# Query projection in half tiles inside the linear attention block, modulation slabs inside the attention projection

## The chip, the cores and the metric

One core of one Trainium2 chip runs the whole program in one launch. The metric is the device time in microseconds (us) of that core. TensorE (PE in the profile) multiplies, VectorE (DVE) and ScalarE (ACT) work elementwise, GpSimd (POOL) too, and SyncE (SP) issues most DMAs. Each engine runs its own queue of instructions in order; semaphores are the only order between queues.

## What is computed

Two layers over 640 tokens (512 latent, 128 context), model width 1024. Of one layer, as the reference has it, this matters here:

```python
mod = jax.nn.silu(cond) @ p['w_mod'][l] + p['b_mod'][l]
sh1, sc1, g1, sh2, sc2, g2 = jnp.split(mod, 6, axis=-1)
h = rms_norm(x, p['norm1'][l]) * (1.0 + sc1) + sh1
(gq, gk, gv, lq, lk, lv, lr, lgo, dq, dk, dv, merge) = split_columns(h @ p['w_in'][l])
gq = rms_norm(gq.reshape(b, n, GQA_HEADS, HEAD_DIM), p['gqa_q_norm'][l])   # gk, dq, dk likewise, then rotary
# A: grouped-query attention of gq, gk, gv; C: differential attention of dq, dk, dv
# B: gated linear attention of lq, lk, lv in chunks of 64 tokens, both directions:
#    state' = decay * state + k_to_end^T v;  out = (masked q_dec k_inv^T) v + q_dec state
gla_out = rms_norm(o_gla, p['gla_out_norm'][l]) * jax.nn.silu(lgo)
mixed = sum_i(sigmoid(merge_i) * (branch_i @ w_branch_i)) @ p['w_out'][l]
x = x + g1 * mixed          # then h from norm2, sc2, sh2; SwiGLU FFN; x = x + g2 * ffn
```

## The kernel before

Every product is made in three passes: a weight slab (2048 columns wide, 1 MB) is loaded into one of two slots of `raw`, ScalarE copies it to a rounded high part `wH`, VectorE subtracts to get the low part `wL`, and TensorE multiplies low activation by high weight, high by low and high by high. The program goes in blocks with a barrier of all engines between them: `head` (or `tail` of the layer before), then per layer `gla`, `project_attention`, `attention`, `merge`, `tail`.

`gla` does the chunked linear attention. The work is four units (`UNITS`: two head pairs by two directions) and, over them, ten steps a (head pair a // 5, token tile a % 5). TensorE first transposes the decayed keys (L703), ScalarE copies them to rows (`g_ker`, L652). `state_steps(u)` (L719) makes the chunk increments of unit u in PSUM banks 0 to 2, and VectorE's `chain(u)` (L825) runs the recurrence over them. `scores(a)` (L736), VectorE's `mask(a)` (L838), `outputs(a)` (L748, L760), VectorE's `out(a)` (L845) make one token tile. ScalarE takes squares (L668) and the square root, VectorE multiplies by the gate (`gate`, L862). TensorE's queue is written out by hand: scores(a + 1), outputs(a), with the four state steps, and in between eight modulation slabs `mod` (L419: 1 MB of `w_mod` each, the columns for g1 and sh2) and four `turn`s (L776) that bring two slabs' rows to columns; ScalarE copies the rows (L660), VectorE adds the bias (L439). After step 9, TensorE runs five half tiles of the first query slab (`row_part`, L344: 4 of 8 contraction tiles, 12 matmuls 512 wide) into banks 0 to 4; their slab is split during step 8 (L308, L313), the second one at the end (L697, L898).

`project_attention` (L903) projects nine slabs s = 0 to 8 (gq halves 0 and 1, dq halves 2 and 3, gk and gv together 4, dk halves 5 and 6, dv halves 7 and 8); s = 0 is already done. A part-1 slab completes five token tiles, which ScalarE copies from PSUM (L1014). Seven `units` of heads are normalised and rotated: ScalarE `squares(q)` (L998, L1003), VectorE `norm(q)` (L1043 to L1078). TensorE transposes them (L1116, table `turns`), ScalarE copies them back (L1024). `high` (L280) and `low` (L286) split the slab ahead. All four queues are loops over s, so what stands later in a step waits for all that is ahead of it: VectorE does low(s + 1), then the norms of `units_at[s]` = {1: (0), 2: (1), 3: (2), 4: (3, 4), 6: (5), 7: (6)}; ScalarE does high(s + 1), the copies of the five tiles, then the squares. At the start, SP spills the residual x to HBM (L945, 2.5 MB), and ScalarE's queue issues the rope tables and the caches; GpSimd makes eight products of the tables, which norm 0 waits for.

Of the kernel before, what the change touches and what calls it, by code (L numbers as in the profile page):

```python
# [21 lines left out]
F32 = mybir.dt.float32  # L22
# [3 lines left out]
ALU = mybir.AluOpType  # L26
# [92 lines left out]
class Stages:  # L119


    def __init__(self, nc, ctx):
# [57 lines left out]
        self.gmod = [at(f"gmod{j}", [P, KT, W256], x) for j, x in enumerate((61440, 69632, x0 + 51200))]  # L180
        self.gmrow = at("gmrow", [P, 512], x0 + 59392)
        self.g_s = [at(f"g_s{u}", [P, NCH, P], x) for u, x in enumerate((77824, 94208, 86016, 104448))]
        self.g_ker = at("g_ker", [P, 4, TT, P], x1)
# [401 lines left out]
MOD_BUF = [1, 0, 2, 1, 0, 2, 1, 2]  # L585


def load_gla_mod(sp, m, d, L, j, sem):
    sp.dma_start(m.gmod[MOD_BUF[j]][:, :, :], k_tiles(d["w_mod"], L, (8 + j) * W256, W256)).then_inc(sem, 16)


def gla(nc, m, d, L, nxt, ahead):
# [10 lines left out]
    with m.block() as block:  # L603
        @block.sync
        def _(sp):
            def load(j):
                load_gla_mod(sp, m, d, L, j, m.sem(f"mod_loaded{MOD_BUF[j]}"))

            def store(u):
                hp, dr = UNITS[u]  # L610
                sp.wait_ge(m.sem("state_done"), u + 1)
                sp.dma_start(d["new_state_gla"][0, ds(L, 1), dr, 2 * hp:2 * hp + 2, :, :].
                             rearrange("a h k e -> (a h k) e"), m.g_s[u][:, blank[dr], :]
                             ).then_inc(m.sem(f"state_out{u // 2}"), 16)

            for j in range(ahead):
                sp.sem_inc(m.sem(f"mod_loaded{MOD_BUF[j]}"), 16)
# [6 lines left out]
            for j in (3, 4, 5):  # L624
                sp.wait_ge(m.sem("slab_used"), j - 2)
                load(j)
            store(0)
            store(1)
            next_load(sp, m, nxt, 0, "slab_used", 5)
            for j in (6, 7):  # L630
                sp.wait_ge(m.sem("slab_used"), j - 1)
                load(j)
            next_load(sp, m, nxt, 1, "slab_used", 7)
            store(2)
            store(3)
            next_loaded(sp, m, nxt)
            next_load(sp, m, nxt, 2, "next_low", 1)
            sp.wait_ge(m.sem("next_loaded2"), nxt[2])
            sp.wait_ge(m.sem("state_out0"), 32)
            sp.wait_ge(m.sem("state_out1"), 32)  # L640
# [8 lines left out]
        def _(act):  # L649
            for u in range(4):  # L650
# [5 lines left out]
            def rows(p):  # L656
                act.wait_ge(m.sem("slab_used"), 2 * p + 2)
                if p:
                    act.wait_ge(m.sem("mod_turned"), p)
                nc.scalar.activation(m.gmrow[:, :], m.ps[:, 3, :], ACT.Copy).then_inc(m.sem("mod_rows"), 1)  # L660
# [16 lines left out]
            rows(0)  # L677
            squares(0, 0)
            squares(0, 1)
            rows(1)  # L680
            squares(0, 2)
            squares(0, 3)
            rows(2)
            squares(0, 4)
            std(0)
            act.wait_ge(m.sem("state_out0"), 32)
            next_high(nc, m, act, nxt, "o_done", 5)
            squares(1, 0)
            squares(1, 1)
            rows(3)  # L690
            for tt in range(2, TT):
                squares(1, tt)
            std(1)
            act.wait_ge(m.sem("next_loaded1"), nxt[2])
            act.wait_ge(m.sem("o_done"), 2 * TT)
            act.wait_ge(m.sem("state_out1"), 32)
            nc.scalar.activation(m.wH[:, 1, :], m.raw[:, 1, :], ACT.Copy).then_inc(m.sem("next_high"), 1)  # L697

        @block.tensor
        def _(pe):  # L700
# [65 lines left out]
            def mod(p):  # L766
                if p:
                    pe.wait_ge(m.sem("mod_added"), p)
                for j in (2 * p, 2 * p + 1):
                    pe.wait_ge(m.sem(f"mod_loaded{MOD_BUF[j]}"), 16 * (MOD_BUF[:j + 1].count(MOD_BUF[j])))  # L770
                    mod_groups(nc, m, m.gmod[MOD_BUF[j]], 3, (j % 2) * W256).then_inc(m.sem("slab_used"), 1)

            def turn(p):
                pe.wait_ge(m.sem("mod_rows"), p + 1)
                for t in range(4):
                    last = nc.tensor.matmul(m.ps[:, 3, 2 * t:2 * t + 2], m.gmrow[:, t * P:(t + 1) * P], m.sel[:, :],  # L776
                                            start=True, stop=True)
                last.then_inc(m.sem("mod_turned"), 1)
# [19 lines left out]
            for tt in range(TT):  # L798
                for sem, count in {0: (("state_done", 4), ("a_masked", 2 * TT)), 3: (("mod_added", 4),),
                                   4: (("o_summed", 2 * TT),)}.get(tt, ()):  # L800
                    pe.wait_ge(m.sem(sem), count)
                wh, wl = (w[:, 0, :].rearrange("p (k c) -> p k c", c=512) for w in (m.wH, m.wL))
                last = row_part(nc, m, wh, wl, tt, tt, 512, 0)
            last.then_inc(m.sem("next_half_done"), 1)

        @block.vector
        def _(dve):
# [40 lines left out]
            def add_mod(p):  # L848
                dve.wait_ge(m.sem("mod_turned"), p + 1)
                add_mod_bias(nc, m, L, 3, 16 + 4 * p, 4).then_inc(m.sem("mod_added"), 1)  # L850
# [44 lines left out]
            for tt in range(TT):  # L895
                gate(1, tt)
            dve.wait_ge(m.sem("next_high"), 2)
            nc.vector.tensor_tensor(m.wL[:, 1, :], m.raw[:, 1, :], m.wH[:, 1, :].bitcast(F32), ALU.subtract  # L898
                                    ).then_inc(m.sem("next_low"), 1)
            dve.wait_ge(m.sem("next_half_done"), 1)  # L900


def project_attention(nc, m, d, L):  # L903


    WIDE = 512
    slabs = [(C_GQ, WIDE, 0), (C_GQ, WIDE, 1), (C_DQ, WIDE, 0), (C_DQ, WIDE, 1), (C_GK, W256, 1),
             (C_DK, WIDE, 0), (C_DK, WIDE, 1), (C_DV, WIDE, 0), (C_DV, WIDE, 1)]
    n = len(slabs)
# [10 lines left out]
    units_at = {1: (0,), 2: (1,), 3: (2,), 4: (3, 4), 6: (5,), 7: (6,)}  # L920
# [14 lines left out]
    def load(sp, d, s, slot, sem):  # L935
        c0, cols, part = slabs[s]
        load_w_rows(sp, m, d, L, c0, cols, part, slot, sem)

    with m.block() as block:
        @block.sync  # L940
        def _(sp):
            out = m.sem("kv_stored")
            took_loads(sp, m)
            sp.sem_inc(m.sem("slab_loaded0"), 16)
# [19 lines left out]
            sp.wait_ge(m.sem("x_spilled"), 16)  # L964
# [11 lines left out]
        def _(act):  # L976
# [12 lines left out]
            def high(s):  # L989
                high_part(nc, m, act, s % 2, 16 * (s // 2 + 1), consumed(s - 2) if s > 1 else None)  # L990

            act.sem_inc(m.sem("high_ready"), 2)
# [14 lines left out]
            for s in range(n):  # L1007
                if 0 < s < n - 1:
                    high(s + 1)
                for tt in range(TT):  # L1010
                    t = 5 * group[s] + tt
                    if slabs[s][2]:
                        act.wait_ge(m.sem("tile_done"), t + 1)
                        nc.scalar.activation(place(s)[:, :, tt, :],  # L1014
                                             m.ps[:, t % 6, 0:slabs[s][1]].rearrange("p (b c) -> p b c", c=P),
# [20 lines left out]
        def _(dve):  # L1036
            order = Signal(m.sem("dve_order"))
            dve.sem_inc(m.sem("low_ready"), 2)  # L1038
# [44 lines left out]
            for s in range(n):  # L1083
                if 0 < s < n - 1:
                    low_part(nc, m, dve, s + 1, (s + 1) % 2)
# [4 lines left out]
        def _(pe):  # L1090
            turn = 0
            pe.sem_inc(m.sem("half_done"), 1)
            for s in range(1, n):
                pe.wait_ge(m.sem("low_ready"), s + 1)
                _, cols, part = slabs[s]
                for tt in range(TT):
                    t = 5 * group[s] + tt
                    if t >= 6:
                        pe.wait_ge(m.sem("tile_copied"), t - 5)
# [2254 lines left out]
```

## Time and profile before

| | |
|---|---|
| median of 3 runs | 2462.07 us (2461.62 to 2463.23) |
| profiled execution, span from first to last instruction | 2464.2 us |
| granted TensorE clock, mean | 0.980 |
| TensorE busy | 2354.2 us (96%) |
| VectorE, ScalarE, GpSimd busy | 1498.5, 1074.1, 218.1 us |
| DMA, mean | 91 GB/s |
| `gla`, layer 0 and layer 1 | from 151.4 and 1363.1 us to the projection's first matmul at 224.4 and 1431.2 |
| `project_attention`, layer 0 | 224.4 to 344.0 us |

The span leaves out what lies around the instructions of the execution; the page gives no other time of its own for it, and it lies 2.1 us above the median of the runs. A timeline row is: start in us, length in us, engine, line, operation, output<-input, shape, count, and in brackets the idle time of the engine before it and what ended it. A granted clock of 1.00 is 2.4 GHz, 0.50 is 1.2 GHz.

### The profile page before, as it was taken

Reading aid. Unit: us, or ns where it says so; the run is one execution under the profiler, and the core shown is the slowest. Engines: PE = TensorE matmul, PEld = TensorE weight load, DVE = VectorE, ACT = ScalarE, POOL = GpSimd, SP = SyncE. Lnnn points to the kernel's source line nnn. Section 1 sums busy time; section 2 is a strip of 40 time slices with the busy share of each in tenths; the row PEclk is TensorE's granted clock in tenths of the full one; section 3 lists DMA queues with packets and bytes.
Section 4 is the critical chain, followed back from the end, with each engine's and each line's share of the span. In section 5 each row is a group of like instructions: output and inputs, shape, how many; then the busy total and the mean of one; then the engine's idle time right before and its main releaser. Section 6 shows DMA issues by size and latency. Waiting matters only on the chain. (4 is left out here: it accounts for less than half of the span.)

```text
span 2464.2 us, 41036 instructions
## 1 busy us (share of the span) xinstructions
PE 2354.2 (96%) x16478; PEld 2181.3 (89%) x16478; DVE 1498.5 (61%) x2400; ACT 1074.1 (44%) x2129; POOL 218.1 (9%) x176
## 2 busy tenths in 40 slices
PE   6989989999999999999999899898999999999998
PEld 5867867789999899999998678677999989999998
DVE  3334656766665773755653446586776568557473
ACT  3533346744442552533435233576444335335252
POOL 1241000000002100000134110000000040000000
PEclk8989999999999999999999999999999999999999
DMA  8235223022225122332231441301222342323222
GB/s 244 88 99 182 70 87 129 27 70 77 89 83 184 48 86 69 86 103 69 78 102 54 148 144 38 102 1 43 78 78 78 111 129 77 96 69 96 59 82 82
DMA packets 248747, 224.03 MB, mean 91 GB/s; under 512 B 9040, under 2 KB 234384, under 8 KB 248048
## 3 DMA queue, kind: packets, MB, share of 16 engines
q1 hardware_dynamic: 242240, 218.59, 28.2%
q10 hardware_dynamic: 5808, 2.17, 0.4%
q8 instruction: 132, 2.16, 0.4%
q0 software_dynamic: 512, 0.66, 0.3%
q14 instruction: 55, 0.45, 0.1%
HBM read 211.70 MB, written 9.70 MB: 90 GB/s over the span
## 5 line engine op out<-in xcount | busy, mean ns | idle before, releaser
L2267 ACT ACTIVATE ring_high<-raw 128x512 fp32r<-128x512 f32 (+1 forms) x278 | 158.1, 609 | 254.0 <-PE ps L2626 146.6
L2411 DVE TENSOR_TENSOR ring_low<-raw,ring_high 128x512 fp32r<-128x512 f32 (+1 forms) x278 | 204.9, 763 | 74.1 <-ACT ring_high L2267 70.0
L2699 PE MATMUL ps<-hH,ring_low 128*128 128x320 f32 x640 | 197.9, 309 | 0.3
L2699 PE MATMUL ps<-hL,ring_high 128*128 128x320 f32 x640 | 197.8, 309 | 0.0
L2699 PE MATMUL ps<-hH,ring_high 128*128 128x320 f32 x640 | 197.8, 309 | 0.0
L1482 DVE SCALAR_TENSOR_TENSOR xT<-ps,mod,xT 128x512 f32<-128x512 f32 (+1 forms) x128 | 64.0, 546 | 189.2 <-PE ps L2626 189.2
L344 PE MATMUL ps<-wH,hL 128*128 128x512 f32 (+1 forms) x460 | 174.5, 379 | 4.8 <-DVEq L1038 3.6
L344 PE MATMUL ps<-wH,hH 128*128 128x512 f32 (+1 forms) x460 | 171.6, 373 | 0.0
L2626 PE MATMUL ps<-gH,ring_low 128*128 128x320 f32 x704 | 160.9, 310 | 0.3 <-DVE xT L1482 0.3
L2626 PE MATMUL ps<-gL,ring_high 128*128 128x320 f32 x704 | 160.4, 309 | 0.0
L2626 PE MATMUL ps<-gH,ring_high 128*128 128x320 f32 x704 | 160.4, 309 | 0.0
L2699 PE MATMUL ps<-t_high,ring_low 128*128 128x320 f32 x480 | 148.5, 309 | 1.8 <-ACT f_p L2315 1.8
L2699 PE MATMUL ps<-t_high,ring_high 128*128 128x320 f32 x480 | 148.3, 309 | 0.0
L2699 PE MATMUL ps<-t_low,ring_high 128*128 128x320 f32 x480 | 148.3, 309 | 0.0
L344 PE MATMUL ps<-wL,hH 128*128 128x512 f32 (+1 forms) x400 | 147.7, 369 | 0.0
L1382 DVE TENSOR_REDUCE a_st<-ps 128x2 f32<-128x1280 f32 x64 | 95.2, 1487 | 46.7 <-PE ps L1234 46.5
L2699 PEld LDWEIGHTS ps<-hH,ring_low 128*128 128x128 f32 x640 | 120.1, 188 | 0.7 <-issue 0.7
L2699 PEld LDWEIGHTS ps<-hH,ring_high 128*128 128x128 f32 x640 | 120.1, 188 | 0.0
L2699 PEld LDWEIGHTS ps<-hL,ring_high 128*128 128x128 f32 x640 | 120.1, 188 | 0.0
L2626 PEld LDWEIGHTS ps<-gH,ring_low 128*128 128x128 f32 x704 | 117.5, 188 | 0.5 <-DVE xT L1482 0.5
L2626 PEld LDWEIGHTS ps<-gL,ring_high 128*128 128x128 f32 x704 | 117.7, 188 | 0.0
L2626 PEld LDWEIGHTS ps<-gH,ring_high 128*128 128x128 f32 x704 | 117.7, 188 | 0.0
(381 smaller groups left out, 6307.8 us busy)
## 6 DMA issues: line engine op xcount, KB each, us to landing
raw<-in_w_in SPq DMA_DIRECT2D x56, 1024.0 KB, 5.2
raw<-in_w_ffn_in SPq DMA_DIRECT2D x88, 512.0 KB, 5.1
gmod<-in_w_mod SPq DMA_DIRECT2D x16, 1024.0 KB, 6.4
modw<-in_w_mod SPq DMA_DIRECT2D x16, 1024.0 KB, 5.3
raw<-in_w_ffn_out SPq DMA_DIRECT2D x16, 1024.0 KB, 5.3
b_raw<-in_w_branch SPq DMA_DIRECT2D x22, 512.0 KB, 3.9
head_w<-in_w_mod SPq DMA_DIRECT2D x8, 1024.0 KB, 12.3
raw<-in_w_out SPq DMA_DIRECT2D x8, 1024.0 KB, 6.3
```

The lines of the kernel that those rows point to most:

```text
L344: last = nc.tensor.matmul(m.ps[:, bank, 0:cols], tok(a[:, k0 + k, :], tt), w[:, k, :], start=(k0 + k == 0 and q == 0), stop=(k0 + k == KT ...
L1382: ins = nc.vector.tensor_reduce(m.a_st[:, s, 0:2], both(s), AX.X, ALU.max, negate=True)
L1482: ins = nc.vector.scalar_tensor_tensor(out=seg, in0=src[c], scalar=g, in1=seg, op0=ALU.mult, op1=ALU.add)
L2267: nc.scalar.activation(ring_block(m.ring_high, b, src.shape[1], src.shape[2]), src, ACT.Copy).then_inc(m.sem("w_high"), 1)
L2411: nc.vector.tensor_tensor(ring_block(m.ring_low, b, nk, cols), src, ring_block(m.ring_high, b, nk, cols).bitcast(F32), ALU.subtract).then_ ...
L2626: last = nc.tensor.matmul(m.ps[:, bank + h, 0:HALF], w[:, kk, :], a[:, k, h * HALF:(h + 1) * HALF], start=(k == 0 and q == 0), stop=(k == ...
L2699: last = nc.tensor.matmul(m.ps[:, plan.banks[n, 0][BANK[what]], 0:HALF], w[:, k, :], a[:, k, :], start=(first and k == 0 and q == 0), stop ...
```

## The change

The modulation slabs and their turns leave `gla` for `project_attention`. In their place, both halves of the first query slab pair (s = 0 and 1) run in `gla`, one half tile after each scores: `q_half(h)` is token tile h // 2, contraction half h % 2, all in PSUM bank 3, copied out by ScalarE's `q_rows`. Slabs 0 and 1 are loaded ahead of the block (in layer 0 only slab 0) and split at its start; slabs 2 and 3 are split at its end and slab 4 loaded. The projection begins with s = 2, has its tiles in banks 0 to 4 and the modulation in bank 5. The spill of x moves to the block before `gla`, so that x's memory can hold the states in `gla` and the modulation slabs in the projection.

```diff
 def gla
         @block.sync
-            for j in range(ahead, 3):
-                load(j)
...
+            for s in range(ahead, 2):
+                load_attention_slab(sp, m, d, L, s, m.sem(f"slab_loaded{s}"))
+            for s in (2, 3, 4):
+                sp.wait_ge(m.sem("slab_low"), s - 1)
+                load_attention_slab(sp, m, d, L, s, m.sem(f"slab_loaded{s}"))
+                if s == 3:
+                    for u in range(4):
+                        store(u)
+            sp.wait_ge(m.sem("slab_loaded4"), 16)
+            sp.wait_ge(m.sem("state_out"), 64)
         @block.scalar
+            def slab_high(s):
+                act.wait_ge(m.sem(f"slab_loaded{s}"), 16)
+                if s >= 2:
+                    act.wait_ge(m.sem("q_half_done"), 9 + s - 2)
+                nc.scalar.activation(m.wH[:, s % 2, :], m.raw[:, raw_slot(s), :], ACT.Copy).then_inc(m.sem("slab_high"), 1)
+
+            def q_rows(tt):
+                act.wait_ge(m.sem("q_half_done"), 2 * tt + 2)
+                nc.scalar.activation(m.rq[:, 0:4, tt, :], m.ps[:, 3, :].rearrange("p (b c) -> p b c", c=P), ACT.Copy
+                                     ).then_inc(m.sem("q_copied"), 1)
...
+            ker_rows(0)
+            ker_rows(1)
+            slab_high(0)
+            ker_rows(2)
+            ker_rows(3)
+            slab_high(1)
+            q_rows(0)
+            for a in range(2 * TT):
+                if a in (1, 3, 5, 7):
+                    q_rows((a + 1) // 2)
+                if a == 7:
+                    slab_high(2)
+                elif a == 8:
+                    slab_high(3)
+                squares(a // TT, a % TT)
+                if a % TT == TT - 1:
+                    std(a // TT)
         @block.tensor
+            def q_half(h):
+
+
+                tt, part = h // 2, h % 2
+                if h < 2:
+                    pe.wait_ge(m.sem("slab_low"), h + 1)
+                if part == 0:
+                    if tt:
+                        pe.wait_ge(m.sem("q_copied"), tt)
+                    else:
+                        pe.wait_ge(m.sem("ke_rows"), 2)
+                wh, wl = (w[:, part, :].rearrange("p (k c) -> p k c", c=512) for w in (m.wH, m.wL))
+                row_part(nc, m, wh, wl, tt, 3, 512, part).then_inc(m.sem("q_half_done"), 1)
 
             state_steps(0)
             scores(0)
-            mod(0)
-            turn(0)
+            q_half(0)
             state_steps(1)
+            q_half(1)
             for a in range(2 * TT):
                 if a + 1 < 2 * TT:
                     scores(a + 1)
+                if a < 8:
+                    q_half(a + 2)
                 outputs(a)
...
-                if a in (1, 3, 6):
-                    mod((1, 3, 6).index(a) + 1)
-                elif a in (2, 4, 7):
-                    turn((2, 4, 7).index(a) + 1)
-            pe.wait_ge(m.sem("next_low"), 1)
...
         @block.vector
+            slab_low(0)
             chain(0, range(9))
             mask(0)
-            add_mod(0)
+            slab_low(1)
             chain(1, range(9))
...
                 out(a)
-                if a in (2, 4, 7):
-                    add_mod((2, 4, 7).index(a) + 1)
-                elif a == 8:
-                    next_low(nc.vector, m, dve, nxt)
+                if a == 8:
+                    slab_low(2)
             gate(0, 4)
             done = inverse(1)
             dve.wait_ge(*done)
             for tt in range(TT):
                 gate(1, tt)
...
+            slab_low(3)
 def project_attention
-    units_at = {1: (0,), 2: (1,), 3: (2,), 4: (3, 4), 6: (5,), 7: (6,)}
+    units_at = {2: (0, 1), 3: (2,), 4: (3, 4), 6: (5,), 7: (6,)}
+    mod_at, turn_at = {(2, 0): 0, (2, 2): 1, (4, 0): 2, (4, 2): 3, (5, 0): 4, (5, 2): 5, (7, 0): 6, (7, 2): 7}, (2, 4, 5, 7)
         @block.sync
-            sp.dma_start(d["x_spill"], flat(m.xT[:, :, :])).then_inc(m.sem("x_spilled"), 16)
-            for s in range(3, n):
+            load_mod(0)
+            load_mod(1)
+            for s in range(5, n):
                 sp.wait_ge(m.sem("low_ready"), s - 1)
-                load(sp, d, s, s % 2, m.sem(f"slab_loaded{s % 2}"))
+                load_attention_slab(sp, m, d, L, s, m.sem(f"slab_loaded{raw_slot(s)}"))
+                for j in {5: (2, 3), 6: (4, 5), 7: (6, 7)}.get(s, ()):
+                    sp.wait_ge(m.sem("mod_used"), j - 1)
+                    load_mod(j)
         @block.scalar
-            for s in range(n):
-                if 0 < s < n - 1:
+            for s in range(begin, n):
+                if begin < s < n - 1:
                     high(s + 1)
                 for tt in range(TT):
                     t = 5 * group[s] + tt
+                    if s in turn_at and tt == 3:
+                        mod_rows(turn_at.index(s))
         @block.vector
+            for s in range(begin, n):
+                if begin < s < n - 1:
+                    low(s + 1)
+                if s - 1 in turn_at:
+                    p = turn_at.index(s - 1)
+                    dve.wait_ge(m.sem("mod_turned"), p + 1)
+                    add_mod_bias(nc, m, L, 5, 16 + 4 * p, 4).then_inc(m.sem("mod_added"), 1)
                 for q in units_at.get(s, ()):
                     norm(q)
         @block.tensor
+            def mod(j):
+                if j and j % 2 == 0:
+                    pe.wait_ge(m.sem("mod_added"), j // 2)
+                pe.wait_ge(m.sem(f"mod_loaded{j % 2}"), 16 * (j // 2 + 1))
+                mod_groups(nc, m, m.gmod[j % 2], 5, j % 2 * W256).then_inc(m.sem("mod_used"), 1)
...
+                    if (s, tt) in mod_at:
+                        mod(mod_at[s, tt])
+                    elif s in turn_at and tt == 4:
+                        turn_mods(turn_at.index(s))
```

## Rows read from the trace of the kernel before

**Rows 1.** The page's part 1: busy time, share of span, instructions of each engine.
```profile
PE 2354.2 (96%) x16478; PEld 2181.3 (89%) x16478; DVE 1498.5 (61%) x2400; ACT 1074.1 (44%) x2129; POOL 218.1 (9%) x176
```

**Rows 2.** Waits of TensorE, 60 to 350 us (layer 0): total, times, longest.
```profile
PE ps L1227 <- PEq L263: 5.4, 1, 5.4
PE ps L419 <- DMA gmod<-in_w_mod: 4.5, 2, 3.1
PE ps L748 <- DVE g_s L825: 2.3, 1, 2.3
```

**Rows 3.** The same waits, 1300 to 1560 us (layer 1).
```profile
PE ps L748 <- DVE g_s L825: 2.8, 1, 2.8
```

**Rows 4.** Timeline of TensorE, layer 0, last outputs and query half tiles: start, length, idle before.
```profile
208.20 0.28 PE L760 MATMUL ps<-g_s,u 64*64 64x128 f32 x2
...
209.08 0.50 PE L344 MATMUL ps<-wH,hL 128*128 128x512 f32 x1 [0.60 <-DVE wL L313]
...
224.43 0.47 PE L344 MATMUL ps<-wH,hL 128*128 128x512 f32 x1 [1.45 <-DVEq L1038]
```

**Rows 5.** Stretches of TensorE: length, busy (x), granted clock, DMA share, GB/s.
```profile
159.00:160.00 1.00, 0.19 (x4) 0.65 1.09 361
...
176.00:177.00 1.00, 1.00 (x10) 0.82 0.00 0
```

**Rows 6.** The same timeline earlier in the block: one length of each kind.
```profile
182.87 1.37 PE L719 MATMUL ps<-lv,g_ker 64*64 64x128 f32 x40 [0.43 <-DVE g_s L825]
184.17 1.05 PE L776 MATMUL ps<-sel,gmrow 128*128 128x2 f32 x8
185.15 0.49 PE L736 MATMUL ps<-u,u 64*128 64x128 f32 x4
...
185.80 1.16 PE L748 MATMUL ps<-lv,g_am 128*128 128x128 f32 x8
...
187.48 1.93 PE L419 MATMUL ps<-gmod,sc 128*32 128x256 f32 x32
```

**Rows 7.** Timeline of ScalarE: row copies and a wide copy; last row layer 1.
```profile
152.15 2.49 ACT L652 ACTIVATE g_ker<-ps 128x640 f32<-128x640 f32 x4 [1.72 <-PE ps L703]
...
194.62 1.89 ACT L308 ACTIVATE wH<-raw 128x2048 fp32r<-128x2048 f32 x1
...
1363.91 1.33 ACT L652 ACTIVATE g_ker<-ps 128x640 f32<-128x640 f32 x2 [2.42 <-PE ps L703]
```

**Rows 8.** Timeline of VectorE, layer 0: first and last wide work after the last copies.
```profile
206.75 2.28 DVE L313 TENSOR_TENSOR wL<-raw,wH 128x2048 fp32r<-128x2048 f32 x1
...
213.87 2.29 DVE L898 TENSOR_TENSOR wL<-raw,wH 128x2048 fp32r<-128x2048 f32 x1
```

**Rows 9.** Timeline of VectorE, layer 0: first state chain and the mask behind it.
```profile
155.10 2.65 DVE L825 SCALAR_TENSOR_TENSOR g_s<-g_s,g_dec,ps 128x128 f32<-128x128 f32 x7 [21.80 <-PE ps L719]
...
158.25 0.72 DVE L838 COPY_PREDICATED g_am<-g_cst,ps 128x512 f32<-128x512 int32 x1
```

**Rows 10.** The page's part 6: DMA issues, KB each, median us to landing.
```profile
raw<-in_w_in SPq DMA_DIRECT2D x56, 1024.0 KB, 5.2
```

**Rows 11.** Timeline of TensorE, layer 1: first matmul of the projection.
```profile
1431.19 0.47 PE L344 MATMUL ps<-wH,hL 128*128 128x512 f32 x1 [2.13 <-DVEq L1038]
```

**Rows 12.** Landing times of the modulation slabs' DMAs, from the view of their tile.
```profile
DMA to landing us min/median/max: 5.1/6.4/10.1
```

**Rows 13.** Stretches of TensorE behind two barriers, columns as in the fifth group.
```profile
1434.00:1436.00 2.00, 2.00 (x6) 0.53 1.07 451
...
353.00:354.00 1.00, 0.99 (x5) 0.57 1.08 362
```

**Rows 14.** Timeline of VectorE in the projection of layer 0: norm 2, low parts.
```profile
269.88 1.49 DVE L1043 TENSOR_REDUCE r_st<-r_sq 128x20 f32<-128x1280 f32 x1 [7.90 <-ACT r_sq L998]
...
278.44 2.29 DVE L286 TENSOR_TENSOR wL<-raw,wH 128x2048 fp32r<-128x2048 f32 x1
...
294.73 2.29 DVE L286 TENSOR_TENSOR wL<-raw,wH 128x2048 fp32r<-128x2048 f32 x1
```

More of the change, by code:

```diff
@@ L179, in __init__ @@
         self.g_e = [at(f"g_e{i}", [P, T], x1 + 2560 * i) for i in range(2)]
[L180 to L183, printed above, removed]
+        self.gmod = [at(f"gmod{j}", [P, KT, W256], 8192 * j) for j in range(2)]
+        self.gmrow = at("gmrow", [P, 512], 16384)
+        self.g_s = [at(f"g_s{u}", [P, NCH, P], 5120 * u) for u in range(4)]
+        self.g_ker = at("g_ker", [P, 4, TT, P], x0 + 51200)
         self.g_am = at("g_am", [P, 2, 2, 2, P], x1 + 10240)
@@ L582, in gate_scale, with attention_slabs, raw_slot, load_attention_slab @@
     nc.gpsimd.tensor_tensor(ki, m.lT[:, 2 + hp, :], ek, ALU.mult).then_inc(done, 1)
[L585 to L592, printed above, removed]
+def attention_slabs():
+    WIDE = 512
+    return [(C_GQ, WIDE, 0), (C_GQ, WIDE, 1), (C_DQ, WIDE, 0), (C_DQ, WIDE, 1), (C_GK, W256, 1),
+            (C_DK, WIDE, 0), (C_DK, WIDE, 1), (C_DV, WIDE, 0), (C_DV, WIDE, 1)]
+def raw_slot(s):
+    return (s + 1) % 2
+def load_attention_slab(sp, m, d, L, s, sem):
+    c0, cols, part = attention_slabs()[s]
+    load_w_rows(sp, m, d, L, c0, cols, part, raw_slot(s), sem)
+def spill_x(sp, m, d):
+    sp.dma_start(d["x_spill"], flat(m.xT[:, :, :])).then_inc(m.sem("x_spilled"), 16)
+def gla(nc, m, d, L, ahead):
     run = [list(range(0, 7)) + [8, 9], list(range(7, 0, -1)) + [9, 8]]
@@ L613, in store @@
                              rearrange("a h k e -> (a h k) e"), m.g_s[u][:, blank[dr], :]
-                             ).then_inc(m.sem(f"state_out{u // 2}"), 16)
-            for j in range(ahead):
-                sp.sem_inc(m.sem(f"mod_loaded{MOD_BUF[j]}"), 16)
+                             ).then_inc(m.sem("state_out"), 16)
+            for s in range(ahead):
+                sp.sem_inc(m.sem(f"slab_loaded{s}"), 16)
             for u, (hp, dr) in enumerate(UNITS):
@@ L649, in _, with ker_rows @@
         def _(act):
-            for u in range(4):
+            def ker_rows(u):
                 act.wait_ge(m.sem("ke_turned"), u + 1)
@@ L846, in out, with slab_low @@
                                       m.ps[:, 4:6, 0:P]).then_inc(m.sem("o_summed"), 1)
-            def add_mod(p):
-                dve.wait_ge(m.sem("mod_turned"), p + 1)
-                add_mod_bias(nc, m, L, 3, 16 + 4 * p, 4).then_inc(m.sem("mod_added"), 1)
+            def slab_low(s):
+                dve.wait_ge(m.sem("slab_high"), s + 1)
+                if s >= 2:
+                    dve.wait_ge(m.sem("q_half_done"), 9 + s - 2)
+                nc.vector.tensor_tensor(m.wL[:, s % 2, :], m.raw[:, raw_slot(s), :], m.wH[:, s % 2, :].bitcast(F32),
+                                        ALU.subtract).then_inc(m.sem("slab_low"), 1)
             def inverse(hp):
@@ L1092, in _, with turn_mods @@
             pe.sem_inc(m.sem("half_done"), 1)
-            for s in range(1, n):
+            pe.sem_inc(m.sem("tile_done"), TT)
+            def mod(j):
[3 more added lines that the diff above has]
+                mod_groups(nc, m, m.gmod[j % 2], 5, j % 2 * W256).then_inc(m.sem("mod_used"), 1)
+            def turn_mods(p):
+                pe.wait_ge(m.sem("mod_rows"), p + 1)
+                for t in range(4):
+                    last = nc.tensor.matmul(m.ps[:, 5, 2 * t:2 * t + 2], m.gmrow[:, t * P:(t + 1) * P], m.sel[:, :],
+                                            start=True, stop=True)
+                last.then_inc(m.sem("mod_turned"), 1)
+            for s in range(begin, n):
                 pe.wait_ge(m.sem("low_ready"), s + 1)
@@ L1097, in _ @@
                     t = 5 * group[s] + tt
-                    if t >= 6:
-                        pe.wait_ge(m.sem("tile_copied"), t - 5)
+                    if slabs[s][2] == 0 or slabs[s][1] == W256:
+                        pe.wait_ge(m.sem("tile_copied"), t - 4)
                     wh = m.wH[:, s % 2, :].rearrange("p (k c) -> p k c", c=cols)
                     wl = m.wL[:, s % 2, :].rearrange("p (k c) -> p k c", c=cols)
-                    last = row_part(nc, m, wh, wl, tt, t % 6, cols, part)
+                    last = row_part(nc, m, wh, wl, tt, t % TT, cols, part)
                     if part:
```

128 lines of the change are left out of this document (34 added, 94 removed).

## The prediction

> **What bounds the kernel now.** I read the page's busy times first: TensorE is busy 96% of the span [rows 1], so a change pays only where TensorE waits, or where it runs below its full clock. I then listed who TensorE waited for around the edited blocks. In layer 0 it loses 4.5 us to modulation slabs still in flight, 2.3 us to the first state chains and 5.4 us to the barrier behind the attention projection [rows 2]; in layer 1 the state chains cost 2.8 us [rows 3]. The barrier between the linear attention block (`gla`) and `project_attention` costs 1.45 us [rows 4]. These idle times, and one stretch in layer 0 in which the granted clock is down from 159.6 to 176.2 us [rows 5], are about all there is to win. The rest is the same work in another place.
>
> **Prices.** In the TensorE timeline of layer 0, next start minus start gives: a state step 1.30 us, a turn of modulation rows 0.98, scores 0.65, outputs 1.68, two modulation slabs 1.87 to 1.93 (0.95 each) [rows 6]. The five half tiles of the first query slab start at 209.08 and end 1.45 us before 224.43 [rows 4]: 13.9 us with a slow first one, so 2.73 each. ScalarE's 2048-wide copy to the high part takes 1.89, 1.85 until the next can start [rows 7]. VectorE's matching subtraction takes 2.28, next start after 2.20 [rows 8].
>
> **Moved work.** TensorE's columns stay the same in all. In `gla`, 8 slab products and 4 turns go (8 x 0.95 + 4 x 0.98 = 11.5 us) and five second halves of query tiles come (5 x 2.73 = 13.65). In the projection it is the reverse. So from the projection's first matmul (call it t0) to its end, work is 13.65 - 11.5 = **2.15 us less per layer**; whether `gla` absorbs it is the next sum.
>
> **`gla`, from its start to t0.** The chain that sets the pace is ScalarE, VectorE, TensorE. From the first row copy of the decayed keys: two copies 1.3 (four take 2.49 [rows 7]), `slab_high(0)` 1.85, `slab_low(0)` 2.2, then only now the state chain of unit 0, 3.15 (from 155.10 to the mask at 158.25 [rows 9]), mask 0.65, `slab_low(1)` 2.2, then on TensorE `q_half(1)` 2.73, scores 0.65, `q_half(2)` 2.73: 17.5 us until the first outputs. `scores(0)` waits behind `slab_high(0)` for the fourth row copy, but inside this chain. Slab 1 of layer 0 is issued after the four state loads and takes some 5.2 us [rows 10], so it is there before ScalarE needs it. The first outputs start at 152.15 + 17.5 = 169.7 in layer 0, and at 1363.91 + 17.5 = 1381.5 in layer 1 [rows 7].
> From there TensorE is continuous: 8 x 1.68 + 2 x 1.47 outputs, 8 x 0.65 scores, 7 x 2.73 half tiles, 2 x 1.30 state steps, and the 0.6 us it already waits before the last outputs: 43.9 us. The mask, chain and copy latencies are covered by a half tile each; take the half tile away and they stand open again.
> Then comes a part without cover. In the kernel before, VectorE's tail after TensorE's last outputs is hidden under five half tiles: TensorE ends its last outputs at 208.48 [rows 4] while VectorE works to 213.87 + 2.29 = 216.16 [rows 8]. The new kernel has the same tail in the same order (`slab_low(2)`, gates, last copy, ten gates, `slab_low(3)`), but nothing is left on TensorE beside it: 7.7 us become idle, and then the barrier, 1.45 in layer 0 and 2.1 in layer 1. SP's wait for slab 4, issued after `slab_low(2)`, ends about 0.5 us earlier than VectorE and costs nothing; were it slower it would add up to 2.
> t0 becomes 169.7 + 43.9 + 7.7 + 1.45 = 222.7 in layer 0 (before 224.43: **-1.7**) and 1381.5 + 43.9 + 7.7 + 2.1 = 1435.2 in layer 1 (before 1431.19 [rows 11]: **+4.0**).
>
> **The projection's start.** SP now issues modulation slabs 0 and 1 only here, and TensorE wants slab 0 after one half tile. Landing takes 5.1, 6.4 or 10.1 us (least, median, most) [rows 12]. I take 6.4, since r_tab, the caches and two more megabytes are in flight too. TensorE's first half tile needs 2.73 at full clock but some 4.8 at half, and after an idle time of 9 us I expect half clock; the two losses overlap. The slab's product ends at 7.5 instead of 3.7: **+3.8** (bounds 2.4 and 7.4). In layer 1 the kernel before already lost 1.7 us to a half clock after this barrier (first row of [rows 13]), which is credited.
>
> **Norms 0 and 1.** They used to have a slab between them and the transposes. Now ScalarE queues `mod_rows(0)`, which waits for TensorE's second slab product (t0 + 13.9), ahead of `squares(0)`. One norm is 278.44 - 269.88 = 8.56 us on VectorE [rows 14]. So norm 0 runs from t0 + 15.8 to 24.4, norm 1 to 33.0. TensorE has the first transposes due at 23.0 (waits 1.4), the second at 27.8 but behind ScalarE's queue of the second standard deviation, `high(4)` and two copies, ready at 29.2 (waits 1.4), the third at 32.7 (0.4): **+3.2** (0 to 6). VectorE's rope tables come 17.6 us after t0 in layer 0 at present, just in time; later tables push all of this.
>
> **The product of slab 4 behind VectorE's queue.** `mod(4)` at (5, 0) waits for `mod_added` 2. VectorE adds that bias in its step s = 5, after norm 2, `low(5)`, norm 3, norm 4 and `low(6)`. In the trace norm 2 starts at 269.88 and `low(6)` ends at 294.73 + 2.29 = 297.02: 27.1 us [rows 14]. Norm 2 starts 2.0 us after the last tile of slab 3, so the bias is there 29.3 us after it. TensorE gets there after five 256-wide tiles (14.4, as many columns as half tiles of 2.73 and a little more), two slab products (1.9), a turn (1.0), two sets of transposes (1.3) and one half tile (2.7): 21.2 us. It waits **8.1 us**, and behind it on its queue stands all the rest of the projection. In the idle time of 5.4 us behind the projection [rows 2] the clock fell, and it came back only at 353.6, 4.2 us after work resumed at 349.35 (second row of [rows 13]); that costs 2.1 at half rate. I take 2.0, bounds 0 and 2.1: **+10.1**. I found no other new wait: `mod(2)` and `mod(6)` need biases that VectorE adds early in its steps, and loads 2 to 8 are issued 10 us or more ahead. The spill of x moves to an earlier block, where SP's next slab has over 10 us in layer 0 and some 4 in layer 1 before ScalarE needs it; I put it at 0 (up to 2).
>
> **Sum.** Layer 0: -1.7 - 2.15 + 3.8 + 3.2 + 10.1 = +13.3. Layer 1: +4.0 - 2.15 + 3.8 - 1.7 + 3.2 + 10.1 = +17.3. Together +30.6 us on the profiled span of 2464.2. The median of the runs is 2462.07, 2.1 below that span; I add the difference to the median: **2493 us**.
>
> **The rivals.** *(B) The wait at slab 4 is not there* (the VectorE queue is less full than I read, or TensorE comes later by itself). For it: every other wait ahead delays TensorE, but it also delays norm 2 by as much. Then 30.6 - 20.2 = +10: 2473.
> *(C) The gaps really fill.* If half tiles cover `gla`'s idle time and keep the clock up, and VectorE's queues cost no more than before, TensorE's work being the same, each layer wins its idle time in `gla` (about 9 and 7 us), and layer 0 also half of the 12 us that TensorE is busy at half clock [rows 5]: 2462 - 16 - 6 = 2440. It needs the 7.7 us tail to be hidden, and I see nothing that hides it; it decides from a tail under 2 us and no wait at `mod(4)`.
> *(D) The clock stays down in `gla`'s front.* Before, one idle time of 3.1 us put TensorE at half rate at 159.6, and it stayed there for 16 us in spite of work in most of them. The new front has several idle times of 0.4 to 1.6 us between 155 and 164. If it is at half rate from `q_half(0)` to the first outputs, three half tiles, a state step and two scores double: +10.8, of which about 3 fall into waits: +8 per layer, 2508. The Trainium skill's page "TensorE: Matmul & The Clock Gate", in "What's actually happening", says that the throttled rate is the default and activity releases it. By that rule the long idle times that I forecast before t0 and at `mod(4)` both end in half rate, which both rows of [rows 13] bear out; whether the short ones of the new front do no run here shows, and the rule speaks for D there.
> *(E) Nothing to measure.* The moved work balances and the waits lie in slack that I misjudged: 2462.
>
> **How the numbers follow.** Forecast A 0.58, with its own range from its bounds 2480 to 2507; B 0.15; C 0.06; D 0.16; E 0.05. About 0.2% (5 us) is what a measurement of this kernel can tell from no change. Faster is C, 0.06; same is E, 0.05; slower is the rest, 0.89. The range reaches down to B (2471) and up to D (2509), and leaves out C, E and the tails.
>
> **What would show it.** In the profile after: TensorE idle 9 to 10 us before the projection's first matmul, ended by the barrier, with VectorE's gates and `slab_low(3)` running in it; the modulation slab product waiting for a DMA near t0 + 5; transposes in slab 3 waiting for VectorE and ScalarE, some 3 us in all; one wait of about 8 us ahead of a slab product, in both layers, ended by VectorE's bias add, with the granted clock at 0.5 behind it. The queues in `gla` should show no wait for a modulation slab. The forecast is wrong if the wait for the bias add is under 3 us, or if TensorE's idle time before t0 is under 4.

## The result and the profile after

The changed kernel takes 2508.14 us (median of 4 runs, 2504.01 to 2510.27) against 2462.65 for the kernel before in the same comparison: a ratio of 1.0183, 95% interval 1.0168 to 1.0197. A second set of runs of the same kernel gave 2507.95 us, ratio 1.0189 (1.0173 to 1.0204). It is slower by 45 us, or 1.8%.

The page of the profiled execution, whose own time was 2510.27 us: span, busy times, and the rows of part 2 for TensorE and its clock (40 slices of 62.7 us, in tenths).

```profile
span 2508.0 us, 41030 instructions
...
PE 2358.4 (94%) x16478; PEld 2174.3 (87%) x16478; DVE 1500.9 (60%) x2400; ACT 1074.2 (43%) x2129; POOL 215.9 (9%) x176
...
PE   6997899989999999999999978898999999999998
...
PEclk8998999999999999999999989999999999999999
```

TensorE is busy for 2358.4 us where it was 2354.2 [rows 1]; the span is 43.8 us longer. So some 40 of the 43.8 us are idle time of TensorE and only 4 us more busy time, and the slices that became weaker are the fourth and fifth (188 to 313 us) and the twenty-fourth and twenty-fifth (1442 to 1567 us), in the edited blocks of the two layers.

Who TensorE waited for in layer 0, from 60 to 350 us (in total, times, longest):

```profile
PE ps L344 <- ACTq L998: 14.9, 1, 14.9
PE ps L419 <- DVE mod L439: 7.8, 1, 7.8
PE ps L344 <- DVE wL L847: 2.3, 2, 2.0
...
PE ps L741 <- ACT g_ker L656: 1.4, 1, 1.4
PE ps L1153 <- DVE rq L1081: 1.4, 2, 1.1
PE ps L1153 <- ACT rq L1032: 1.3, 1, 1.3
```

The same in layer 1, 1250 to 1620 us:

```profile
PE ps L344 <- ACTq L998: 13.8, 1, 13.8
PE ps L419 <- DVE mod L439: 7.8, 1, 7.8
...
PE ps L344 <- DVE wL L847: 2.0, 1, 2.0
```

The wait for modulation slabs (4.5 us) and the one for the state chains (2.3 and 2.8 us) of [rows 2] and [rows 3] are gone. In their place stand a wait of 14.9 and 13.8 us in front of the projection, where the kernel before waited 1.45 and 2.1 us ([rows 4], [rows 11]), one of 7.8 us ahead of a modulation product in each layer, 2.3 and 2.0 us for the first low parts, and 2.7 us at the transposes of slab 3 (1.4 for VectorE and 1.3 for ScalarE, in both layers; the kernel before waited 0.7 us there).

The times of four matmuls divide the loss, in us: the first of `gla`, the first outputs, the projection's first (t0) and the attention block's first.

| | before, layer 0 | after, layer 0 | before, layer 1 | after, layer 1 |
|---|---|---|---|---|
| `gla` start | 151.37 | 152.21 | 1363.13 | 1381.89 |
| first outputs, from the start | 18.79 | 20.32 | 14.31 | 21.10 |
| t0, from the start | 73.06 | 79.23 | 68.06 | 78.90 |
| t0 to attention | 124.92 | 138.01 | 126.29 | 140.26 |
| both blocks | 197.98 | 217.24 | 194.35 | 219.16 |

The two blocks lose 19.3 and 24.8 us, 44.1 in all. All else together differs by -0.3 us, so neither the spill in the earlier blocks nor anything behind them costs a time that shows.

Busy time times granted clock, in stretches of 0.5 us, is TensorE's work in us at full clock. From t0 to attention it is 118.8 us in both layers after, and 118.9 and 118.8 before. So what these 138.0 and 140.3 us have more than before is idle time (9.6 and 9.8 us) and lower clock (3.6 and 4.2), not work.

The boundary in layer 0, TensorE's timeline (start, length, instructions, idle before):

```profile
172.53 1.05 PE L753 MATMUL ps<-lv,g_am 128*128 128x128 f32 x8
...
216.21 0.28 PE L765 MATMUL ps<-g_s,u 64*64 64x128 f32 x2
...
231.44 0.77 PE L344 MATMUL ps<-wH,hL 128*128 128x512 f32 x1 [14.95 <-ACTq L998]
```

VectorE at the same place:

```profile
214.76 2.28 DVE L847 TENSOR_TENSOR wL<-raw,wH 128x2048 fp32r<-128x2048 f32 x1
...
219.24 2.71 DVE L860 SCALAR_TENSOR_TENSOR glr<-glr,g_st,lg 128x128 f32<-128x128 f32 x10
221.88 2.28 DVE L847 TENSOR_TENSOR wL<-raw,wH 128x2048 fp32r<-128x2048 f32 x1
```

and ScalarE:

```profile
218.66 0.30 ACT L683 ACTIVATE g_st<-g_st,cst 128x10 f32<-128x10 f32 x1
225.20 0.40 ACTq L973 DMA_DIRECT2D r_tab<-in_const_rope  x1
...
226.30 2.54 ACTq L977 DMA_DIRECT2D kv<-in_cache_diff_v  x1
...
230.23 0.94 ACTq L984 DMA_DIRECT2D kv<-in_cache_gqa_k  x2
243.68 0.60 ACT L995 ACTIVATE gmrow<-ps 128x512 f32<-128x512 f32 x1 [24.72 <-PE ps L419]
```

TensorE ends its last outputs at 216.2 + 0.3. VectorE goes on with the second half of its tail until 221.88 + 2.28 = 224.16, which is 7.7 us, as in [rows 8] against [rows 4]. The barrier opens at about 225.2: ScalarE issues its first DMA there. TensorE does not start then but at 231.44, when ScalarE has issued the last of seven DMAs (230.23 + 0.94 = 231.17). The row of waits says so too: "ACTq L998" is the line behind those DMAs, `act.sem_inc(m.sem("tile_copied"), TT)`. TensorE's first tile of the new projection (t = 5) waits for `tile_copied` 1, and this increment alone raises it: the block's own copies come later. In layer 1 the seven issues run from 1456.33 to 1460.52 us, and t0 is at 1460.79.

### The profile page after: what moved, and what is told of

It is laid out like the page before. It is cut to its first block and busy times, and to the rows that moved or that the text cites. A ratio compares the mean times of both kernels' runs of the same rounds, so it can differ in the third digit from the quotient of the medians.

```text
span 2508.0 us, 41030 instructions
## 1 busy us (share of the span) xinstructions
PE 2358.4 (94%) x16478; PEld 2174.3 (87%) x16478; DVE 1500.9 (60%) x2400; ACT 1074.2 (43%) x2129; POOL 215.9 (9%) x176
## 5 line engine op out<-in xcount | busy, mean ns | idle before, releaser
L344 PE MATMUL ps<-wH,hL 128*128 128x512 f32 (+1 forms) x460 | 182.8, 397 | 33.1 <-ACTq L998 28.8
L344 PEld LDWEIGHTS ps<-wH,hL 128*128 128x128 f32 x460 | 89.2, 194 | 57.5 <-issue 36.4
```

The source lines that it names most:

```text
L344: last = nc.tensor.matmul(m.ps[:, bank, 0:cols], tok(a[:, k0 + k, :], tt), w[:, k, :], start=(k0 + k == 0 and q == 0), stop=(k0 + k == KT ...
```

## The experiments

Each kernel is the changed kernel with the edit shown; a time is the median of its runs, compared with 2508.

**The changed kernel once more**, with no edit, for comparison with the last three kernels below.

> The changed kernel as it is, for comparison on the same chip as the runs beside it: 2508 us (2504 to 2510).

Measured: the 2507.95 us given above. From its blocks' starts, t0 comes after 78.9 and 78.7 us and attention another 139.3 and 138.0 us later, where the first profile had 79.2 and 78.9, then 138.0 and 140.3. So the same kernel differs by 1.3 and 2.3 us in one stretch from profile to profile, and a gain of that size in one stretch of one profile is not evidence.

**ScalarE's increments ahead of its DMA issues.**

```diff
         def _(act):
+            act.sem_inc(m.sem("high_ready"), begin + 2)
+            act.sem_inc(m.sem("tile_copied"), TT)
             act.dma_start(m.r_tab[:, :, :, :], d["const_rope"]).then_inc(m.sem("rope_tables"), 16)
...
-            act.sem_inc(m.sem("high_ready"), begin + 2)
-            act.sem_inc(m.sem("tile_copied"), TT)
```

> The changed kernel with one edit: ScalarE raises tile_copied and high_ready at the start of the projection, ahead of its seven DMA issues, instead of behind them. In the trace after, TensorE starts the projection 6.2 us after ScalarE's first DMA issue (225.20 to 231.44) and its wait of 14.9 us is put down to ScalarE's queue. Theory 1: TensorE's first tile waits for that increment, which stands behind the DMA issues; then the wait falls from 14.9 and 13.8 us to about 9.2 to 9.8 in both layers, a wait of at most 1.5 us for modulation slab 0 appears, and the time goes from 2508 to about 2498 (2496 to 2501). Rival: the barrier or VectorE's tail itself is that long, and ScalarE's increment is late for another reason; then the time stays at 2508 within 2 us.

Measured: 2501.40 us (2501.01 to 2501.74), ratio 1.0163 (1.0148 to 1.0178): 6.6 us less. Waits of TensorE in layer 0:

```profile
PE ps L344 <- ACTq L974: 9.2, 1, 9.2
PE ps L419 <- DVE mod L439: 7.8, 1, 7.8
...
PE ps L419 <- DMA gmod<-in_w_mod: 1.1, 1, 1.1
```

and its timeline at the projection's start:

```profile
225.14 0.77 PE L344 MATMUL ps<-wH,hL 128*128 128x512 f32 x1 [9.19 <-ACTq L974]
...
231.71 1.07 PE L419 MATMUL ps<-gmod,sc 128*32 128x256 f32 x16 [1.11 <-DMA gmod<-in_w_mod]
```

The first wait falls from 14.9 to 9.2 us (layer 1: 13.8 to 9.8), which is what the tail and the barrier explain, 7.7 + 1.5 and 7.7 + 2.1. That settles the mechanism, at a price of 5.8 and 4.0 us. (t0 comes 5.7 and 4.8 us earlier from the blocks' starts, but 0.8 of the 4.8 lies in front of the first outputs.) In time less came back than I expected, 6.6 of 10 us: with TensorE earlier, modulation slab 0 is no longer there in time (1.1 and 1.0 us). Where the last 1 us stayed is not shown. The clock, down after the idle time in every one of these kernels, came back 3.2 and 6.0 us after t0 in layers 0 and 1 of the changed kernel, 4.9 and 2.8 us after it in its second profile, and 6.1 and 4.1 us after it here.

**The bias added behind norm 3.**

```diff
-                if s - 1 in turn_at:
-                    p = turn_at.index(s - 1)
-                    dve.wait_ge(m.sem("mod_turned"), p + 1)
-                    add_mod_bias(nc, m, L, 5, 16 + 4 * p, 4).then_inc(m.sem("mod_added"), 1)
+                if s - 1 in turn_at and s != 5:
+                    add_mod(turn_at.index(s - 1))
                 for q in units_at.get(s, ()):
                     norm(q)
+                    if q == 3:
+                        add_mod(1)
```

> The changed kernel with one edit: VectorE adds the second modulation bias right behind norm 3, not behind norm 4 and the low part of slab 6. Theory 1 (as predicted): the wait of 7.8 us ahead of modulation slab 4's product, and the half clock behind it, are VectorE's queue; the wait falls to under 1 us in both layers and the time falls by 2 x (7.3 + up to 2.1), to 2490 (2488 to 2494). Rival: another thing is late next (transposes that wait for norm 3 or 4, ScalarE's rows) and takes the place of the wait; then less than half comes back, 2499 or more.

Measured: 2488.80 us (2488.19 to 2489.11), ratio 1.0111 (1.0096 to 1.0126): 19.2 us less, 9.6 per layer. The waits in layer 0 from the largest on:

```profile
PE ps L344 <- ACTq L998: 14.1, 1, 14.1
PE ps L344 <- DVE wL L847: 2.0, 1, 2.0
PE ps L708 <- PEq L263: 1.6, 1, 1.6
```

The wait for the bias is not in the list any more, and nothing is late in its place: the time lies in the range of theory 1. Of the 9.6 us, 7.8 were the wait; the other 1.8 fit the clock, whose fall in the changed kernel shows in these stretches (length, busy, granted clock, DMA share, GB/s); TensorE goes on at 298.74:

```profile
294.44:295.44 1.00, 0.00 (x0) 1.00 0.00 0
295.44:296.44 1.00, 0.00 (x0) 0.81 0.00 0
299.44:300.44 1.00, 1.00 (x12) 0.50 0.00 0
302.44:303.44 1.00, 1.00 (x5) 0.78 0.94 316
```

Busy time lost to the lower clock behind this wait is 2.1 us in layer 0 and 2.9 in layer 1 of that profile, 2.5 and 2.0 in the second one.

**Two half tiles beside VectorE's tail.**

```diff
-                if a < 8:
+                if a < 6:
                     q_half(a + 2)
                 outputs(a)
...
+            q_half(8)
+            q_half(9)
...
             for tt in range(TT):
                 gate(1, tt)
+            slab_low(2)
             slab_low(3)
```

`slab_high(2)`, `slab_high(3)` and `q_rows(4)` go behind ScalarE's last square root, and slab 4 is loaded at the start of the projection.

> The changed kernel with the last two half tiles moved behind the last outputs, the splits of slabs 2 and 3 behind the gates, and slab 4's load moved into the projection. Theory 1: VectorE's tail of 7.7 us after TensorE's last outputs is idle time of TensorE because nothing is left beside it; with 5.5 us of half tiles beside the gates, block and idle time shrink: TensorE's wait before the projection falls from 14.9 to about 11 us (part of it is ScalarE's late increment, which stays), and the time by 3 to 4 us per layer, to 2501 (2499 to 2504). Rival: what bounds the block's end is the chain of high and low parts, which now starts later, so the time stays within 2 us of 2508 or rises.

Measured: 2498.57 us (2497.26 to 2499.16), ratio 1.0151 (1.0134 to 1.0168): 9.4 us less, somewhat more than the 4 to 9 of theory 1.

```profile
PE ps L344 <- ACTq L997: 10.7, 1, 10.7
PE ps L419 <- DVE mod L439: 7.8, 1, 7.8
```

The idle time falls to 10.7 us (10.5 in layer 1), near the 11 expected. TensorE's last outputs start at 57.3 us from the block's start instead of 62.8, with 5.5 us of half tiles behind them, and VectorE's last low part ends 4.3 us behind those. So the tail was idle time for want of cover. t0 came 4.1 and 4.0 us earlier (75.2 and 74.9 from the start); the other 1.3 us of the 9.4 are open, within what one kernel's profiles differ by.

**Squares of unit 0 first.**

```diff
+                if s == begin:
+                    squares(0)
                 for tt in range(TT):
...
                 for q in units_at.get(s, ()):
-                    if q != 3:
+                    if q not in (0, 3):
                         squares(q)
```

> The changed kernel with one edit: in the projection ScalarE squares unit 0 before it waits for the first modulation rows, so norm 0 starts some 12 us earlier. Theory 1 (as predicted): the waits of the transposes in slab 3 for VectorE and ScalarE (2.7 us in all) come from that order and go in both layers; the wait at modulation slab 4 stays at 7.8 us, since both ends of it are tied to slab 3's last tile. The time falls by 5 us, to 2503 (2501 to 2505). Rival: the wait ahead of modulation slab 4 grows by what TensorE gains here, because VectorE's chain is what sets both; then the time stays at 2508.

Measured: 2500.03 us (2499.29 to 2501.10), ratio 1.0158 (1.0142 to 1.0173): 7.9 us less.

```profile
PE ps L344 <- ACTq L998: 14.7, 1, 14.7
PE ps L419 <- DVE mod L439: 7.8, 1, 7.8
PE ps L344 <- DVE wL L847: 2.0, 1, 2.0
```

No transpose waits in the list, and the wait for the bias is still 7.8 us: both as expected, and the rival falls. The time fell by 2.5 us more than the 5.4 us of these waits, below the range that I had given; the blocks show 2.6 and 4.8 us less from t0 to attention (3.9 and 2.5 against the second profile), and the remainder is not explained by a wait.

**GpSimd's product later.** VectorE's timeline in the changed kernel shows the first low part of the block, the state chain and the second low part:

```profile
156.11 3.86 DVE L847 TENSOR_TENSOR wL<-raw,wH 128x2048 fp32r<-128x2048 f32 x1 [21.98 <-ACT wH L664]
159.90 2.63 DVE L820 SCALAR_TENSOR_TENSOR g_s<-g_s,g_dec,ps 128x128 f32<-128x128 f32 x7
...
163.66 2.27 DVE L847 TENSOR_TENSOR wL<-raw,wH 128x2048 fp32r<-128x2048 f32 x1
```

and GpSimd's:

```profile
152.19 5.63 POOL L649 TENSOR_TENSOR lg<-lg,g_on 128x2560 f32<-128x2560 f32 x1 [6.52 <-POOLq L263]
```

The first subtraction takes 3.86 us, the others 2.28. GpSimd's product ends at 152.19 + 5.63 = 157.82, and the subtraction 2.1 us later.

```diff
+            pool.wait_ge(m.sem("slab_low"), 2)
             nc.gpsimd.tensor_tensor(lg, lg, m.g_on[:, :].unsqueeze(1).broadcast_to([P, 20, P]), ALU.mult
```

> The changed kernel with one edit: GpSimd starts its product of the output gate's gains (5.6 us) only when the low part of slab 1 is made. In the trace after, the first low part of the block runs from 156.11 to 159.97 (3.86 us where all others take 2.28), and GpSimd's product ends at 157.83. Theory 1: VectorE's subtraction stands still until GpSimd's instruction is done (157.83 + 2.1 = 159.97); moved away, it takes 2.3 us in both layers, the first outputs come 1.6 us earlier and the time falls by 3 to 5 us (with less half clock on the first half tile), to 2504. Rival: the subtraction is slow because it is the first one, or because of DMA traffic; then it still takes 3.9 us and the time stays.

Measured: 2505.82 us (2504.26 to 2506.64), ratio 1.0177 (1.0162 to 1.0192), 2.1 us less than the changed kernel beside it (2507.95), where theory 1 had 3 to 5. The two ranges do not overlap, but the intervals of the ratios do, so the gain in time is at the edge of what the runs can tell. What tells the theories apart is the row:

```profile
155.78 2.29 DVE L848 TENSOR_TENSOR wL<-raw,wH 128x2048 fp32r<-128x2048 f32 x1 [21.97 <-ACT wH L665]
157.99 2.64 DVE L821 SCALAR_TENSOR_TENSOR g_s<-g_s,g_dec,ps 128x128 f32<-128x128 f32 x7
```

```profile
164.11 5.71 POOL L650 TENSOR_TENSOR lg<-lg,g_on 128x2560 f32<-128x2560 f32 x1 [18.76 <-DVE wL L848]
```

The subtraction takes 2.29 us in both layers, and the first outputs come 18.8 us after the block's start (layer 1: 19.8), 1.5 and 1.3 us earlier. GpSimd's product now runs beside the state chain, and the chain's steps take as long as before (2.63 us for seven).

**All five edits.**

> The changed kernel with all five edits (increments first, bias early, cover of the tail, squares first, GpSimd later). Theory 1: the five costs lie one behind the other on TensorE's queue and add up: 6.7 + 19.3 + 9.6 + 8.1 + 3 to 5 = 47 to 49 us less than the changed kernel, 2460 (2457 to 2466), level with the kernel before. Rival: some share the same idle time (the late increment and the tail both lie before the projection), so that the sum is smaller by what is counted twice, about 5 to 10 us: 2466 to 2470.

Measured: 2467.56 us (10 runs, 2464.57 to 2468.53), ratio 1.0015 (1.0006 to 1.0024): 40.4 us less than 2507.95. The single gains (6.6, 19.2, 9.4, 7.9, 2.1) sum to 45.2, so 4.8 us are missing. The result lies 6 to 9 us above the sum that theory 1 wrote down and within the rival's. The rival's reason, idle time counted twice before the projection, explains at most a part: t0 from the block's start came 10.1 us earlier in layer 0, where the single edits give 5.4 + 3.7 + 1.5 = 10.6, and 8.3 in layer 1, where they give 4.6 + 3.8 + 1.4 = 9.8 (all against the changed kernel's second profile). Behind t0 there are new losses in layer 0:

```profile
PE ps L344 <- ACTq L974: 5.9, 1, 5.9
PE ps L344 <- DVE wL L848: 1.8, 2, 1.3
PE ps L419 <- DMA gmod<-in_w_mod: 1.7, 1, 1.7
```

Modulation slab 0 is now waited for (1.7 us; 0.7 in layer 1), and the clock was at its lower level twice there, from t0 to 225.8 and from 229.2 to 232.6. How the 4.8 us divide among these is not shown.

**Slab 3 split in the projection.** All edits; in `gla` only slab 2 is split behind the gates, slab 3 at the start of the projection (`high(3)`, `low(3)`, ahead of unit 0's squares and norm), and `mod_at` begins with (2, 1) and (2, 3).

> All five edits, and more taken out of the block's end: slab 3 is split in the projection instead of behind the gates, and the first two modulation products come one tile later. Theory 1: what ends the block then is the low part of slab 2, some 1.5 us behind TensorE's last half tile, so TensorE's idle time before the projection falls to about 3 us, the clock stays up there, and no wait for modulation slab 0 is left: 4 to 6 us less per layer than with the five edits alone, 2452 (2447 to 2458), faster than the kernel before. Rival: the norms now start behind the split of slab 3, and the transposes of slab 3 wait for them again; then at most half of it is won, 2458 or more.

Measured: 2458.46 us (10 runs, 2452.35 to 2459.85), ratio 0.9981 (0.9971 to 0.9991), 9.1 us less than with the five edits.

```profile
PE ps L344 <- ACTq L972: 3.1, 1, 3.1
PE ps L344 <- DVE wL L848: 2.0, 2, 1.5
```

TensorE's idle time before the projection is 3.1 us (3.8 in layer 1), and there is no wait for slab 0 or at the transposes, so the rival's mechanism is not there. The gain lies in the 8 to 12 us of theory 1, but was counted from 2460 and so misses its range by half a microsecond. One part of the theory failed: the clock did not stay up, it was at its lower level until 221.0 and 1429.3 us, 3.2 and 5.8 us after work resumed. This version is 0.19% faster than the kernel before, about the least that a measurement of this kernel can tell, with an interval that excludes 1.

## Why the prediction was right, and where it was not

The forecast was 2493 us, slower, range 2471 to 2509; the time is 2508.14, inside and at its upper end. Several steps were exact, three were mis-sized and one was absent.

- **Moved work, steady steps.** From the first outputs to the last, `gla` takes 42.5 us in both layers; forecast was 43.9 to the end of the last outputs, which last 1.5: the same. Apart from the known 0.6 us before the last outputs, no wait of those steps is in the list.
- **Moved work, the projection.** Forecast 2.15 us less per layer behind t0; measured nothing (118.8 us at full clock against 118.9 and 118.8). The price of 0.95 us for a modulation slab came from slabs that ran in pairs. In the projection each stands alone between half tiles:

```profile
239.50 0.39 PE L344 MATMUL ps<-wH,hH 128*128 128x512 f32 x1
...
242.22 0.39 PE L344 MATMUL ps<-wH,hH 128*128 128x512 f32 x1
242.54 1.07 PE L419 MATMUL ps<-gmod,sc 128*32 128x256 f32 x16
243.54 0.50 PE L344 MATMUL ps<-wH,hL 128*128 128x512 f32 x1
...
246.44 0.39 PE L344 MATMUL ps<-wH,hL 128*128 128x512 f32 x1
```

  Twelve matmuls of 512 columns take 2.72 us (239.50 to 242.22). The thirteen from 242.22 to 246.44 and the slab between them take 4.22 us, where thirteen alone take 2.95: the slab costs 1.27. Eight of these and four turns at 0.98 are 14 us, no less than the 13.65 of the half tiles.
- **VectorE's tail without cover.** Forecast 7.7 us, measured 7.7.
- **The start of the projection: the step that failed.** The sum had t0 at -1.7 and +4.0 us against the kernel before; it came at +6.2 and +10.8 from the block's start. The step "and then the barrier" took TensorE to be free after it. It named VectorE and the DMA as what TensorE waits for there and left out ScalarE, whose queue I had read only for its copies. The increment of `tile_copied` stands in the listing behind seven DMA issues, and the first experiment puts its price at 5.8 and 4.0 us. In the kernel before the same place was harmless, since the first tiles there, up to t = 5, waited for no count of ScalarE.
- **Modulation slab 0.** Forecast +3.8 per layer, half of it a wait for the DMA. There was no such wait: ScalarE's lateness covered it. What remained is the lower clock, back 3.2 and 6.0 us after t0, a loss of 1.6 and 3.0 us. Once the increment is early the wait is there, 1.1 and 1.0 us.
- **The front of `gla`.** Forecast first outputs 18.3 and 18.4 us after the start; measured 20.3 and 21.1. The chain was right in its order, but the term `slab_low(0)` was 2.2 and took 3.8 us, because GpSimd's product ran at the same time (1.5 us by the fifth experiment). The first half tile, at the lower clock, took 4.3 and 5.4 us instead of 2.73. In layer 0 that cost nothing, since TensorE was still early for the second low part:

```profile
165.98 0.50 PE L344 MATMUL ps<-wH,hL 128*128 128x512 f32 x1 [0.29 <-DVE wL L847]
```

  In layer 1 TensorE came 0.8 us behind it. The last 0.4 us are two half tiles of 2.9 us and scores of 0.8 instead of 2.73 and 0.65.
- **Norms 0 and 1.** Forecast 3.2 us, measured 1.4 + 1.3 = 2.7 (2.0 more than before), and gone with the order of ScalarE's queue, as argued.
- **The bias behind VectorE's queue.** Forecast 8.1 us and 2.0 for the clock, measured 7.8 and, from the whole gain of 9.6, 1.8 for the clock. This was the largest term and the one with both ends from rows ([rows 14]).
- **The spill.** Forecast 0; the first matmul of `gla` in layer 0 starts at 150.3 to 152.2 us in nine profiles of the changed kernel and its variants, around the 151.37 of before.

From t0 to attention the forecast was +15.0 and +13.3, measured +13.1 and +14.0. That this fits so well is in part luck: the 2.15 us of work that did not go away stand against 2.2 us in layer 0, and 0.9 in layer 1, that the start of the projection was dearer in the forecast than in the trace. Up to t0 it was 7.9 and 6.8 us short: 5.8 and 4.0 are ScalarE's increment and 2.0 and 2.7 the front of `gla`. These are 14.7 us, against a whole error of 13.5 us in the two blocks and 15 in the time.

Rival D gave 2508, the measured time, by another way: the clock did fall in the front, but for one half tile, not until the first outputs, and it costs nothing in layer 0 and 0.8 us in layer 1, not 8. That its number fits is chance. Rival B is refuted, since its wait is there, and rival E by the 1.8%. Rival C needed the tail hidden, and the last two kernels show what it takes: covering the tail, four changes of order and the split of slab 3 moved, for 0.2%.

## What to carry to other kernels

When work is moved into the gaps of an engine, look at what used to run beside that work: the tail of another engine that it covered stays where it is and becomes idle time. Then read the head of every queue behind each barrier, issues and bare semaphore increments included, and ask of each of them who waits for it now; an increment that stood harmlessly behind DMA issues cost 5.8 and 4.0 us once a matmul needed it. A price read from a run of equal pieces does not hold for one piece between others: 0.95 against 1.27 us here. A helper result that one engine adds "some time later" wants its place in the queue computed from both ends: here the forecast had 29.3 against 21.2 us, and 7.8 us were lost and the clock with them.

## What the runs showed of the hardware

A VectorE subtraction with two inputs in SBUF, begun while GpSimd ran a product of two SBUF operands, took 3.86 and 3.87 us against 2.28. It ended 2.15 us after GpSimd's end, about a whole subtraction later, and took 2.29 us once they were apart. State-chain steps with one input in PSUM ran beside the same product at their usual speed. The Trainium skill's page "SBUF — State Buffer", section "SBUF: two separate sides", calls the port pair that the two engines share an exclusive lock that also holds for a VectorE operation with two SBUF inputs against a GpSimd operation that reads SBUF; these rows agree with it.

After the idle times of 14.9 and 13.8 us before the projection in layers 0 and 1 of the changed kernel, TensorE's clock came back to its upper level 3.2 and 6.0 us after work resumed; in the second profile of the same kernel it was 4.9 and 2.8 us, and in all nine profiles 2.8 to 6.1. So the same wait costs between 1.4 and 3 us in clock in one and the same kernel, and differences of one or two microseconds between these experiments should be read with that in mind.
